# A stick-breaking and forgetting attention, pipelined head by head on one Trainium2 core

## The chip, the cores and the metric

The kernel is one program on one core of a Trainium2 chip. The metric is the device time of one execution in microseconds; less is better. All data are f32.

## The reference

Two transformer blocks run one after the other on 512 tokens of width 1024. The change lies in the attention part of the first block, which is this, cut to what matters:

```python
proj = h @ w_in                  # 8 stick-breaking and 8 forgetting heads of width 64
# stick-breaking head, query block i, keys 0..end
z = q @ k.T * HEAD_DIM ** -0.5
log_keep = where(k < q, log_sigmoid(-z), 0)
later = reverse_cumsum(log_keep) - log_keep
w = where(k < q, exp(log_sigmoid(z) + later), 0)
out = w @ v
# forgetting head: q and k are first rms-normed over the head and scaled by g_q, g_k
z = q @ k.T * HEAD_DIM ** -0.5 + log_f_cum[q] - log_f_cum[k]
out = softmax(where(k <= q, z, -inf)) @ v
x = x + (1 + ga2) * (concat(heads) @ w_o)
```

`log_f_cum` is the running sum of `log_sigmoid(h @ w_f + b_f)`, one row per head. Before this part stands a feed-forward (ffn 0), behind it another (ffn 1); the second block has linear and latent attention and a mixture of experts.

## The kernel before

The normed tokens lie feature-major in `hT` (8 chunks of 128 features x 512 tokens). Each engine has its own program, written out in order; semaphores join them, and nothing but that order and the semaphores sets when work runs. Weights come through six slots of 128x4096 (`slot0` to `slot5`), which SyncE fills in its own order as each slot is freed.

The attention goes by pairs of heads: four stick-breaking pairs, then four forgetting pairs, as two loops of three rounds and one written-out round each. A pair's q, k and v weights take one slot: slot 2 for all stick pairs, slot 3 for all forgetting pairs. Per pair TensorE makes

- q and k (`qk_projection`, L758, 8 products of 512 columns each, into banks 7 and 6 of the accumulator memory `ps`), for the next pair while the second head of a pair is worked on;
- v (L792, 32 products of 128 columns, bank 7), during the first head;

and per head

- the scores of the four query blocks against keys 0..end (L784; banks 0 to 2, 128, 256, 384 and 512 columns). In a forgetting head each of the four is followed by a second product of the same columns that adds the gate sums (L786: rows of ones and of `Fc`, in `FL` and `FR`), and by one of 128 columns that adds the causal mask (L787, the table `after` through the identity);
- ten 128x128 transposes of the weights (L804, banks 3 to 5), copied to `PT` by VectorE (L1602, L1638) and ScalarE (L1255, L1272);
- ten products with v (L820, bank 6), copied to `oT` by VectorE (L1609, L1644).

Between scores and transposes stands, in a stick head, ScalarE's abs, exp, log (L1240 to L1245), VectorE's max, scan and subtract (L1584 to L1596) and ScalarE's exp (L1249, from then on `probs_ready`); in a forgetting head, VectorE's four maxima (L1618), ScalarE's four exps (L1266) and VectorE's reciprocal and four scalings (L1621, L1626). One product of `head_ones` each for q and k (L764, L809), ScalarE's root (L1233), VectorE's reciprocal (L1569) and scaling (L1574) norm q and k of a forgetting pair; all scratch of it is in `buf1`, and q and k have one buffer each (`qT`, `kT`).

Ahead of the pairs the gate projection runs (L832), and all engines meet behind it; they meet again behind the last pair. Then come eight output chunks (L851, 8 products of 512 columns each), each added to `xT` by VectorE (L1657), with the square sums of the next norm between them (L662), and ffn 1 begins (L707).

Of the kernel before, what the change touches and what calls it, by code (L numbers as in the profile page):

```python
# [13 lines left out]
P = 128  # L14
D = 1024
KC = D // P
# [115 lines left out]
def build(nc, a, out):  # L132
    ctx = ExitStack()
    with ctx:
# [38 lines left out]
        qT = part(0, 512)  # L173
        kT = part(512, 512)
        vt = part(1024, 512).rearrange("p (t n) -> p t n", t=4)
        buf1 = part(1536, TRI)
        buf2 = part(1536 + TRI, TRI)
        PT = part(1536 + 2 * TRI, TRI).rearrange("p (b q) -> p b q", q=P)
        oT = part(5376, 4096).rearrange("p (c t) -> p c t", c=8)
        FL = big[:, 9472:9984]  # L180
        FR = big[:, 9984:10496]
        Fc = big[0:8, 10496:11008]
        fA = tmp[0:8, 0, 0:512]
        fB = tmp[0:8, 1, 0:512]
# [29 lines left out]
        s_rs = sem("rstd_ready")  # L214
# [8 lines left out]
        s_qkv = sem("qkv_done")  # L223
        s_qc = sem("q_copied")
        s_kvc = sem("kv_copied")
        s_qsq = sem("qk_squares_ready")
        s_qss = sem("qk_square_sum_done")
        s_qr = sem("qk_rstd_ready")
# [12 lines left out]
        s_fl = sem("forget_ready")  # L241
        s_fm = sem("forget_head_ready")
        s_fp = sem("forget_proj_done")
        s_f1 = sem("forget_exp_ready")
        s_wo = sem("mix_done")
# [253 lines left out]
        def _(sp):  # L499
# [54 lines left out]
            def pairs(s, at):  # L554
                k = u.take(s, 3, 4)[1]
                view = ring[s][:, 0:KC * 384].rearrange("p (k w n) -> p k w n", k=KC, w=3)
                with sp.Fori(0, 4) as i:
                    sp.wait_ge(freed[s], i + k)
                    for w in range(3):
                        sp.dma_start(view[:, :, w], w_in[:, :, bass.ds(at + w * 512 + i * P, P)]).then_inc(filled[s], 16)  # L560

            ffn(0)
            pairs(2, 0)
            pairs(3, 1536)
            for n, s in enumerate((4, 5)):
                sp.wait_ge(freed[s], u.take(s, 1)[1])
                sp.dma_start(ring[s][:, :].rearrange("p (f n) -> p f n", f=4), w_o[:, 4 * n:4 * n + 4, :])\
                    .then_inc(filled[s], 16)
            ffn(1)
# [67 lines left out]
        def _(pe):  # L637
# [111 lines left out]
            def qk_projection(s, have, i, fox, heads):  # L749

                w = ring[s][:, 0:KC * 384].rearrange("p (k w n) -> p k w n", k=KC, w=3)
                pe.wait_ge(filled[s], have + 48 + i * 48)
                for m in range(2):
                    if m == 1:

                        pe.wait_ge(s_o, heads)
                    for k in range(KC):
                        last = mm(ps[:, 7 - m, :], w[:, k, m, :], hT[:, k, META:TOK], start=(k == 0), stop=(k == KC - 1))  # L758
                    last.then_inc(s_qkv, 1)
                if fox:  # L760

                    pe.wait_ge(s_qc, i + 5)
                    pe.wait_ge(s_qsq, 2 * i + 1)
                    mm(ps[:, 7, :], const("head_ones"), buf1[:, 0:512], start=True, stop=True).then_inc(s_qss, 1)  # L764

            def pair(s, have, i, fox, after):

                w = ring[s][:, 0:KC * 384].rearrange("p (k w n) -> p k w n", k=KC, w=3)
                h0 = i * 2 + (8 if fox else 0)
                pr = i + (4 if fox else 0)  # L770
                if fox:
                    pe.wait_ge(s_qn, 2 * i + 2)
                else:
                    pe.wait_ge(s_qc, pr + 1)
                    pe.wait_ge(s_kvc, pr * 2 + 1)
                for hh in range(2):
                    h = h0 + hh
                    lo = hh * HD
                    if fox:
                        pe.wait_ge(s_fm, 2 * i + hh + 1)  # L780
                    for t in range(4):
                        n = P * (t + 1)
                        z = ps[:, [0, 0, 1, 2][t], (P if t == 1 else 0):(P if t == 1 else 0) + n]
                        last = mm(z, qT[lo:lo + HD, t * P:(t + 1) * P], kT[lo:lo + HD, 0:n], start=True, stop=not fox)  # L784
                        if fox:
                            mm(z, FL[lo:lo + HD, t * P:(t + 1) * P], FR[lo:lo + HD, 0:n], start=False, stop=True)  # L786
                            last = mm(z[:, t * P:n], ident, const("after"), start=False, stop=True, skip_group_check=True)  # L787
                    last.then_inc(s_z, 1)
                    if hh == 0:
                        for t in range(4):  # L790
                            for k in range(KC):
                                last = mm(ps[:, 7, t * P:(t + 1) * P], hT[:, k, META + t * P:META + (t + 1) * P], w[:, k, 2, :],  # L792
                                          start=(k == 0), stop=(k == KC - 1))
                        last.then_inc(s_qkv, 1)
                        pe.drain().then_inc(freed[s], 1)
                    elif after:

                        qk_projection(*after, h0 + 2)
                    pe.wait_ge(s_p, h + 1)
                    for (q, k), b in BLOCK_AT.items():  # L800
                        at = TILE_AT[q] + k * P
                        dst = ps[:, 3, b * P:(b + 1) * P] if b < 4 else \
                            ps[:, 4 + (b - 4) // 3, (b - 4) % 3 * P:(b - 4) % 3 * P + P]
                        last = nc.tensor.transpose(dst, buf2[:, at:at + P], ident)  # L804
                    last.then_inc(s_pt, 1)
                    if hh == 1 and after and after[3]:
                        pe.wait_ge(s_qsq, 2 * after[2] + 2)
                        pe.wait_ge(s_qstd, 2 * after[2] + 1)
                        mm(ps[:, 7, :], const("head_ones"), buf1[:, 512:1024], start=True, stop=True).then_inc(s_qss, 1)  # L809
                    pe.wait_ge(s_ptc, 2 * h + 2)  # L810
                    if hh == 0:

                        pe.wait_ge(s_kvc, pr * 2 + 2)
                    elif after:

                        pe.wait_ge(s_kvc, pr * 2 + 3)
                    pe.wait_ge(s_o, h + 1)
                    for q in range(4):
                        for k in range(q + 1):
                            last = mm(ps[0:HD, 6, q * P:(q + 1) * P], vt[:, k, lo:lo + HD], PT[:, BLOCK_AT[q, k], :],  # L820
                                      start=(k == 0), stop=(k == q))
                    last.then_inc(s_pv, 1)

# [4 lines left out]

            pe.wait_ge(s_late, 48)
            for k in range(KC):  # L830
                pe.wait_ge(s_hn, KC + k + 1)
                last = mm(ps[0:8, 5, :], wf[:, k, :], hT[:, k, META:TOK], start=(k == 0), stop=(k == KC - 1))  # L832
# [16 lines left out]
            for d in range(KC):  # L849
# [3 lines left out]
                if d >= 2:  # L853

                    norm_sum(2, d - 2)
# [1179 lines left out]
```

## Time and profile before

| | us |
|---|---|
| three runs: lowest, median, highest | 2963.74, 2965.77, 2982.33 |
| the profiled execution, its own time | 2963.49 |
| its span, first to last instruction | 2961.1 |
| TensorE busy | 2585.0 (87%) |
| VectorE busy | 1045.7 (35%) |
| ScalarE busy | 453.6 (15%) |
| GpSimd busy | 179.8 (6%) |
| first product behind the norm ahead of attention | at 543.06 |
| first score product | at 567.14 |
| first output product | at 958.49 |
| first product of ffn 1 | at 1026.87 |

The rows further down are of this one execution. A time of TensorE in a timeline row is the start of the first of xN products and the length to the modelled end of the last; the next row's start tells how long a group really held the engine. A product of one program line is two MATMUL records in f32. The granted clock is 1.00 where the engine ran at 2.4 GHz and 0.50 where it ran at 1.2 GHz.

### The profile page before, as it was taken

How to read it: one execution, taken by the hardware profiler on the slowest of the kernel's cores; microseconds unless marked ns; L12 is line 12 of the kernel's file. 1: busy time of each engine (PE TensorE's matmuls, PEld its weight loads, DVE VectorE, ACT ScalarE, POOL GpSimd, SP SyncE). 2: the span in 40 equal slices, each digit the busy share in tenths (PEclk: the TensorE clock that was granted, in tenths of full speed). 3: DMA queues.
4: the chain of work that ended last, by engine and by line, in shares of the span. 5: the costliest groups of instructions: out<-in, count | busy, mean ns of one | idle time of the engine just before them, and what ended most of it. 6: DMA issues, size and time to landing. Idle time of an engine off the chain costs nothing. (4 is left out here: it accounts for less than half of the span.)

```text
span 2961.1 us, 25080 instructions
## 1 busy us (share of the span) xinstructions
PE 2585.0 (87%) x9179; PEld 1222.8 (41%) x9179; DVE 1045.7 (35%) x1216; ACT 453.6 (15%) x713; POOL 179.8 (6%) x458
## 2 busy tenths in 40 slices
PE   8999999888888999999999789588888888888884
PEld 4444444455565344443444545433333333333331
DVE  3555520333333133331012662433333233233334
ACT  2000000344112100100010221011111111111111
POOL 0000000000000000000000000011111111111111
PEclk9999999998888999999999789799899999899997
DMA  7444532001013012231220100299999999999996
GB/s 260 162 135 155 172 112 61 21 25 39 22 43 113 1 57 85 63 109 39 87 101 29 33 1 22 87 416 415 416 409 411 413 402 412 407 404 415 404 409 241
DMA packets 182825, 563.10 MB, mean 190 GB/s; under 512 B 16864, under 2 KB 132848, under 8 KB 156544
## 3 DMA queue, kind: packets, MB, share of 16 engines
q1 hardware_dynamic: 172384, 554.10, 49.0%
q0 software_dynamic: 10400, 8.42, 0.9%
q8 instruction: 30, 0.49, 0.1%
q14 instruction: 11, 0.09, 0.0%
HBM read 567.19 MB, written 20.97 MB: 199 GB/s over the span
## 5 line engine op out<-in xcount | busy, mean ns | idle before, releaser
L1090 PE MATMUL ps<-slot,xT 128*64 128x512 f32 x2048 | 518.9, 665 | 160.4 <-DMA slot<-in_expert_w_up 159.4
L707 PE MATMUL ps<-hT,slot 128*128 128x512 f32 x1408 | 614.0, 597 | 13.0 <-ACT hT L1184 7.2
L707 PEld LDWEIGHTS ps<-hT,slot 128*128 128x128 f32 x1408 | 267.3, 191 | 351.1 <-issue 348.2
L1090 PEld LDWEIGHTS ps<-slot,xT 128*64 128x64 f32 x2048 | 168.6, 152 | 508.8 <-issue 459.5
L735 PE MATMUL ps<-big,slot 128*128 128x512 f32 x704 | 309.8, 600 | 12.0 <-DVE big L1499 6.2
L1918 DVE COPY hT<-ps 128x256 f32<-128x256 f32 x64 | 27.2, 424 | 630.5 <-PE ps L1098 630.5
L1109 PE MATMUL ps<-slot,hT 128*64 128x512 f32 x1024 | 233.8, 598 | 1.2 <-DVE hT L1918 1.2
L1909 DVE RECIPROCAL xT<-xT 64x512 f32<-64x512 f32 x64 | 214.1, 3345 | 2.2
L735 PEld LDWEIGHTS ps<-big,slot 128*128 128x128 f32 x704 | 135.3, 193 | 182.0 <-issue 168.9
L1495 DVE RECIPROCAL eb<-eb 128x512 f32<-128x512 f32 x44 | 147.5, 3353 | 1.5
L1493 DVE TENSOR_SCALAR eb<-eb 128x512 f32<-128x512 f32 x44 | 18.8, 427 | 331.4 <-ACT eb L1194 331.4
L1378 ACT ACTIVATE xT<-ps 64x512 f32<-64x512 f32 x64 | 37.8, 591 | 596.9 <-PE ps L1090 596.9
L1522 DVE SCALAR_TENSOR_TENSOR xT<-ps,small,xT 128x512 f32<-128x512 f32 x16 | 12.0, 750 | 296.1 <-PE ps L735 296.1
L1972 POOL MEMSET spare<- 1x4 f32 x1 | 0.1, 91 | 1915.8 <-DVEq L456 1915.8
L1109 PEld LDWEIGHTS ps<-slot,hT 128*64 128x64 f32 x1024 | 68.2, 136 | 114.9 <-issue 110.8
L758 PE MATMUL ps<-hT,slot 128*128 128x512 f32 x256 | 111.7, 594 | 0.1
L1384 ACT ACTIVATE hT<-ps 64x512 f32<-64x512 f32 x128 | 75.9, 593 | 201.5 <-PE ps L1109 200.7
L1194 ACT ACTIVATE eb<-ps 128x512 f32<-128x512 f32 x44 | 26.3, 597 | 418.6 <-PE ps L707 418.5
L1171 ACT ACTIVATE tmp<-xT 128x512 f32<-128x512 f32 (+1 forms) x32 | 20.1, 632 | 387.3 <-DVE xT L1522 327.7
L1072 PE MATMUL ps<-cst,xT 64*128 64x64 f32 x512 | 67.1, 272 | 7.5 <-DMA xT<-normed_tokens,tcol 7.5
L758 PEld LDWEIGHTS ps<-hT,slot 128*128 128x128 f32 x256 | 48.0, 190 | 61.5 <-issue 61.5
L820 PE MATMUL ps<-big 128*64 128x128 f32 x320 | 52.9, 339 | 21.5 <-DVE big L1638 8.8
(339 smaller groups left out, 2414.2 us busy)
## 6 DMA issues: line engine op xcount, KB each, us to landing
slot<-in_expert_w_gate SPq DMA_DIRECT2D x64, 2048.0 KB, 17.3
slot<-in_expert_w_up SPq DMA_DIRECT2D x64, 2048.0 KB, 22.5
slot<-in_expert_w_down SPq DMA_DIRECT2D x64, 2048.0 KB, 23.2
slot<-in_w_mod SPq DMA_DIRECT2D x18, 2048.0 KB, 8.0
slot<-in_w_gate SPq DMA_DIRECT2D x22, 1024.0 KB, 5.5
slot<-in_w_up SPq DMA_DIRECT2D x22, 1024.0 KB, 7.9
slot<-in_w_down SPq DMA_DIRECT2D x16, 1408.0 KB, 7.4
slot<-in_w_in SPq DMA_DIRECT2D x24, 512.0 KB, 5.8
```

Source lines behind the costliest of these rows:

```text
L707: last = mm(ps[:, 2 * j + g, :], w[:, g, k, j * P:(j + 1) * P], hT[:, k, META:TOK], start=(k == 0), stop=(k == KC - 1))
L735: last = mm(ps[:, down_bank(d), :], w[:, f, :], aT[:, f, :], start=(f == 0), stop=(f == FC - 1))
L758: last = mm(ps[:, 7 - m, :], w[:, k, m, :], hT[:, k, META:TOK], start=(k == 0), stop=(k == KC - 1))
L820: last = mm(ps[0:HD, 6, q * P:(q + 1) * P], vt[:, k, lo:lo + HD], PT[:, BLOCK_AT[q, k], :], start=(k == 0), stop=(k == q))
L1072: last = nc.tensor.transpose(ps[:, 4 + j, k * CAP:(k + 1) * CAP], xs[j].rearrange("p (m k) -> p k m", k=KC)[:, k, :], ident[0:CAP, 0:CAP])
L1090: last = mm(ps[g * CAP:(g + 1) * CAP, j, :], xsT[j][:, k, :], w[g][:, k, :], start=(k == 0), stop=(k == KC - 1))
L1109: last = mm(ps[g * CAP:(g + 1) * CAP, 2 + j, :], hid[j][:, c, :], w[:, c, g * 512:(g + 1) * 512], start=(c == 0), stop=(c == 3))
L1378: av(sg[j], ps[0:CAP, j, :], ACT.Exp, scale=-1.0).then_inc(s_eg, 1)
L1384: last = av(ys[j][:, g * 512:(g + 1) * 512], ps[g * CAP:(g + 1) * CAP, 2 + j, :], ACT.Copy)
L1495: v.reciprocal(eb[:, j, :], eb[:, j, :]).then_inc(s_vec, 1)
L1909: v.reciprocal(sg[j], sg[j]).then_inc(s_vec, 1)
L1918: v.tensor_copy(hid[j].rearrange("p c s -> p (c s)"), ps[:, 6 + j, 0:4 * CAP]).then_inc(s_hd, 1)
```

## The change

1. TensorE's order goes by heads: transposes of head h, scores of head h+1, products with v of head h, then half of the projections of a coming pair (`first_half` after an odd head, `second_half` after an even one). All sixteen heads are written out; there are no loops left.
2. q, k and v have two buffers each (`qb`, `kb`, `vt`, and `qF`, `kF` in slot 0). ScalarE copies them all. Pairs use slots 2, 1 and 3 in turn.
3. A forgetting head's `qF` and `kF` have 72 rows: 64 of q or k, and 8 of ones or of `Fc` times a column of the identity. The second score product is gone; the mask product stays. q and k are normed from `tmp` with scratch in `eb`, VectorE writing the two heads of a pair apart.
4. The first four of the eight products of output chunks 0 to 5 run in heads 13 and 14 and are added to `xT` there; behind head 15 come chunks 6 and 7 whole and the other four products of 0 to 5.
5. The gate projection stands behind the first scores. The meetings of all engines ahead of the pairs and behind them are gone. Maxima and exps of a forgetting head go tile by tile from the largest, each with its own signal.

The diff, cut to its core:

```diff
+        PAIR_SLOT = [2, 1, 3, 2, 1, 3, 2, 1]
+        MIX_ORDER = (6, 7, 0, 1, 2, 3, 4, 5)
...
-                        last = mm(z, qT[lo:lo + HD, t * P:(t + 1) * P], kT[lo:lo + HD, 0:n], start=True, stop=not fox)
-                        if fox:
-                            mm(z, FL[lo:lo + HD, t * P:(t + 1) * P], FR[lo:lo + HD, 0:n], start=False, stop=True)
-                            last = mm(z[:, t * P:n], ident, const("after"), start=False, stop=True, skip_group_check=True)
...
+            def scores(h):
...
+                else:
+                    pe.wait_ge(s_qn, 2 * (p - 4) + 2)
+                    pe.wait_ge(s_fm, h - 7)
+                    q, k = qF[p % 2][hh], kF[p % 2][hh]
+                for t in range(4):
+                    n = P * (t + 1)
+                    b, at = Z_AT[t]
+                    last = mm(ps[:, b, at:at + n], q[:, t * P:(t + 1) * P], k[:, 0:n], start=True, stop=True)
+                    if p >= 4:
+                        last = mm(ps[:, b, at + t * P:at + n], ident, const("after"), start=False, stop=True, skip_group_check=True)
+                last.then_inc(s_z, 1)
...
+            def first_half(n, heads):
+                pe.wait_ge(filled[PAIR_SLOT[n]], pair_have[n])
+                if n < 4:
+                    pe.wait_ge(s_qc if n == 1 else s_kc, 1 if n == 1 else n)
+                    project(n, 1, 7, 0, 4)
+                    if heads:
+                        pe.wait_ge(s_o, heads + 1)
+                    project(n, 0, 6).then_inc(s_q, 1)
+                else:
...
+                    project(n, 0, 7).then_inc(s_q, 1)
+                    pe.wait_ge(s_o, heads + 1)
+                    project(n, 1, 6).then_inc(s_k, 1)
+                    pe.wait_ge(s_qsq, 2 * (n - 4) + 1)
+                    pe.wait_ge(s_qc, n + 1)
+                    mm(ps[:, 7, :], const("head_ones"), eb[:, 0, :], start=True, stop=True).then_inc(s_qss, 1)
...
+            def second_half(n, heads):
+                if n < 4:
+                    project(n, 1, 7, 4, KC).then_inc(s_k, 1)
+                else:
+                    pe.wait_ge(s_qsq, 2 * (n - 4) + 2)
+                    pe.wait_ge(s_qstd, 2 * (n - 4) + 1)
+                    mm(ps[:, 7, :], const("head_ones"), eb[:, 1, :], start=True, stop=True).then_inc(s_qss, 1)
+                pe.wait_ge(s_o, heads + 1)
+                values(n, 6)
...
+            for h in range(N_HEAD):
+                p = h // 2
+                turn(h)
+                if h + 1 < N_HEAD:
+                    scores(h + 1)
+                else:
+                    pe.drain().then_inc(freed[0], 1)
+                head_out(h)
+                if h % 2 and p + 2 < N_PAIR:
+                    first_half(p + 2, h + 1)
+                elif not h % 2 and p + 1 < N_PAIR:
+                    second_half(p + 1, h + 1)
+                elif h < 15:
...
+                        mix(d, bank, 0, 4).then_inc(s_wo, 1)
...
+            for j, d in enumerate(MIX_ORDER):
+                mix(d, j, 0 if d >= 6 else 4, 8).then_inc(s_wo, 1)
```

VectorE's new order, by head:

```diff
+            for h in range(N_HEAD):
+                p, n = h // 2, h + 1
+                turned_out(h)
+                if n < 8:
+                    head_copy(h)
+                    log_weights(n)
+                if h % 2 == 0 and 4 <= p + 1 < N_PAIR:
+                    inverse(p + 1, 0)
+                if n >= 8:
+                    if n < N_HEAD:
+                        masked_max(n)
+                    head_copy(h)
+                    if n < N_HEAD:
+                        forget_probs(n)
...
+                if h % 2 == 0 and 4 <= p + 1 < N_PAIR:
+                    normed(p + 1, 0)
+                    inverse(p + 1, 1)
+                    normed(p + 1, 1)
```

TensorE's order in the loop over stick pairs, before. L784 are scores, L792 v, L804 transposes, L820 products with v, L758 q and k of the next pair:

```order
L792 MATMUL ps<-slot2,hT 128x128 x32
L804 MATMUL ps<-cst,big 128x128 [waits probs_ready]
L804 MATMUL ps<-cst,big 128x128 x9
...
L820 MATMUL ps<-big 64x128 [waits heads_copied,kv_copied]
L820 MATMUL ps<-big 64x128 x9
L784 MATMUL ps<-big 128x128
L784 MATMUL ps<-big 128x256
L784 MATMUL ps<-big 128x384
L784 MATMUL ps<-big 128x512
...
L758 MATMUL ps<-hT,slot2 128x512 [waits filled2]
```

And of the change, from the transposes of head 1 on (L802 transposes, L791 scores of head 2, L820 products with v of head 1, L767 half of k and all of q of pair 2):

```order
L802 MATMUL ps<-cst,big 128x128 [waits probs_ready]
L802 MATMUL ps<-cst,big 128x128 x9
L791 MATMUL ps<-slot 128x128 [waits k_copied,q_copied]
L791 MATMUL ps<-slot 128x256
L791 MATMUL ps<-slot 128x384
L791 MATMUL ps<-slot 128x512
L820 MATMUL ps<-big 64x128 [waits v_copied,probs_turned_copied]
L820 MATMUL ps<-big 64x128 x9
L767 MATMUL ps<-hT,slot 128x512 [waits k_copied,filled3]
L767 MATMUL ps<-hT,slot 128x512 x3
L767 MATMUL ps<-hT,slot 128x512 [waits heads_copied]
L767 MATMUL ps<-hT,slot 128x512 x7
```

The scores have moved from behind the products with v to ahead of them, and every head now has projections between its scores and its transposes.

VectorE's order from the work on head 7's weights to the maxima of head 8, in the change (L1611 to L1619 are `log_weights(7)`, L1649 and L1656 norm q and k of pair 4, L1638 and L1645 are copies of head 7's transposes and output, L1625 the maxima of head 8):

```order
L1611 SCALAR_TENSOR_TENSOR big<-ps,big 128x768 [waits softplus_ready]
L1614 SCALAR_TENSOR_TENSOR big<-ps,big 128x512
L1616 SCALAR_TENSOR_TENSOR big<-cst,big 128x1280 [waits vector_step]
L1617 TENSOR_TENSOR big<-ps,big 128x768 [waits vector_step]
L1619 TENSOR_TENSOR big<-ps,big 128x512
L1649 RECIPROCAL eb<-eb 128x512 [waits qk_std_ready]
L1656 SCALAR_TENSOR_TENSOR slot<-tmp,gqs,eb 64x512 [waits q_copied,vector_step]
L1656 SCALAR_TENSOR_TENSOR slot<-tmp,gqs,eb 64x512
L1649 RECIPROCAL eb<-eb 128x512 [waits qk_std_ready]
L1656 SCALAR_TENSOR_TENSOR slot<-tmp,cols,eb 64x512 [waits k_copied,vector_step]
L1656 SCALAR_TENSOR_TENSOR slot<-tmp,cols,eb 64x512
L1638 TENSOR_TENSOR big<-ps,cst 128x512 [waits probs_turned]
```

Before, the norms of this pair stood behind the copy of head 7's transposes; now they stand ahead of it, and each scaling is two instructions of 64 rows in the place of one of 128.

## Rows read from the trace of the kernel before

**Rows 1.** Busy time of each engine in four stretches, with TensorE's granted clock (PEclk).

```profile
core 0: us, PE busy (x) PEld busy (x) DVE busy (x) ACT busy (x) POOL busy (x), PEclk, DMA share, GB/s
567.10:697.80 130.70, 108.18 (x517) 75.06 (x517) 47.02 (x47) 55.28 (x53) 0.00 (x0) 0.90 0.19 48
749.10:957.50 208.40, 182.07 (x796) 120.94 (x796) 70.85 (x121) 40.31 (x93) 0.00 (x0) 0.86 0.20 63
...
749.10:771.20 22.10, 21.84 (x88) 15.69 (x88) 4.89 (x13) 2.15 (x8) 0.00 (x0) 0.62 0.00 1
775.90:797.20 21.30, 21.30 (x60) 10.17 (x60) 5.36 (x13) 3.23 (x10) 0.00 (x0) 1.00 0.12 29
```

**Rows 2.** Waits of TensorE from 552 to 1018: us in total, times, longest.

```profile
PE ps L804 <- ACT big L1249: 21.1, 4, 5.3
...
PE ps L784 <- DVE big L1574: 6.0, 3, 4.8
...
PE ps L804 <- issue: 0.8, 3, 0.3
```

**Rows 3.** Timeline of TensorE: gate projection, then the first stick pair.

```profile
543.06 9.19 PE L832 MATMUL ps<-hT,wf 128*8 128x512 f32 x16 [5.83 <-ACT hT L1184]
...
567.14 2.42 PE L784 MATMUL ps<-big 64*128 64x128 f32 x8 [0.79 <-DVE big L1560]
569.49 7.41 PE L792 MATMUL ps<-slot,hT 128*128 128x128 f32 x64
582.17 2.40 PE L804 MATMUL ps<-cst,big 128*128 128x128 f32 x10 [5.27 <-ACT big L1249]
585.65 3.71 PE L820 MATMUL ps<-big 128*64 128x128 f32 x20 [1.09 <-ACT big L1255]
589.29 2.42 PE L784 MATMUL ps<-big 64*128 64x128 f32 x8
```

**Rows 4.** Timeline of VectorE and ScalarE in head 0's chain.

```profile
574.81 0.96 DVE L1584 SCALAR_TENSOR_TENSOR big<-ps,big 128x768 f32<-128x768 f32 x1 [7.73 <-ACT big L1245]
...
580.85 1.27 ACT L1249 ACTIVATE big<-big 128x1280 f32<-128x1280 f32 x1 [4.77 <-DVE big L1596]
```

**Rows 5.** Timeline of TensorE around a forgetting head's scores.

```profile
749.13 0.79 PE L784 MATMUL ps<-big 64*128 64x128 f32 x2 [4.79 <-DVE big L1574]
...
773.62 2.37 PE L820 MATMUL ps<-big 128*64 128x128 f32 x20 [1.10 <-ACT big L1272]
775.91 0.48 PE L784 MATMUL ps<-big 64*128 64x128 f32 x2
...
782.59 13.90 PE L758 MATMUL ps<-hT,slot 128*128 128x512 f32 x32
796.32 1.02 PE L764 MATMUL ps<-big,cst 128*128 128x512 f32 x2
797.18 1.25 PE L804 MATMUL ps<-cst,big 128*128 128x128 f32 x10
```

**Rows 6.** Groups between 540 and 1045: busy us, mean ns; idle before.

```profile
L792 PEld LDWEIGHTS ps<-slot,hT 128*128 128x128 f32 x512 | 61.1, 201 | 3.0 <-issue 3.0
...
L1569 DVE RECIPROCAL big<-big 128x512 f32<-128x512 f32 x8 | 26.8, 3349 | 8.7 <-ACT big L1233 8.7
...
L1574 DVE SCALAR_TENSOR_TENSOR big<-big,gqs 128x512 f32<-128x512 f32 x4 | 3.0, 739 | 0.0
```

**Rows 7.** Timeline of VectorE: the last step of head 9's weights.

```profile
786.90 1.28 DVE L1626 TENSOR_SCALAR big<-big,fox_s 128x128 f32<-128x128 f32 x4
```

**Rows 8.** Timeline of TensorE: the outputs' start and that of ffn 1.

```profile
958.49 20.86 PE L851 MATMUL ps<-big,slot 128*128 128x512 f32 x48 [0.88 <-DVEq L456]
...
1026.87 30.32 PE L707 MATMUL ps<-hT,slot 128*128 128x512 f32 x64 [5.83 <-ACT hT L1184]
```

**Rows 9.** DMA queues of instructions, 552 to 1018, and a wait without releaser.

```profile
q8 instruction: 7, 0.11, 0.1%
q14 instruction: 3, 0.02, 0.0%
...
PEld ps L784 <- issue: 10.4, 20, 5.0
```

More of the change, by code:

```diff
@@ L568, in _ @@
                     .then_inc(filled[s], 16)
+            u.take(0, 0)
             ffn(1)
@@ new lines, in mix @@
+            def mix(d, bank, f0, f1):
+                for f in range(f0, f1):
+                    if f == 7:
+                        pe.wait_ge(s_o, N_HEAD + 1)
+                    last = mm(ps[:, bank, :], wo[f // 4][:, f % 4, d * P:(d + 1) * P], oT[:, f, :], start=(f == f0), stop=(f == f1 - 1))
+                return last
+            pe.wait_ge(filled[PAIR_SLOT[0]], pair_have[0])
+            for k in range(KC):
+                pe.wait_ge(s_hn, KC + k + 1)
+                last = mm(ps[:, 7, :], pair_w[0][:, k, 0, :], hT[:, k, META:TOK], start=(k == 0), stop=(k == KC - 1))
@@ L846, in _ @@
-            for n, s in enumerate((4, 5)):
-                pe.wait_ge(filled[s], u.take(s, 1)[0] + 16)
-            phase_left(pe, 7)
-            for d in range(KC):
-                for f in range(8):
-                    last = mm(ps[:, d, :], wo[f // 4][:, f % 4, d * P:(d + 1) * P], oT[:, f, :], start=(f == 0), stop=(f == 7))
-                last.then_inc(s_wo, 1)
-                if d >= 2:
-                    norm_sum(2, d - 2)
+            first_half(1, 0)
+            pe.wait_ge(s_f1, 1)
@@ L1284, in _ @@
+            for n in (5, 6, 7):
+                phase_left(act, n)
             norm(2)
@@ new lines, in inverse, with normed @@
+            def inverse(p, m):
+                dve.wait_ge(s_qstd, 2 * (p - 4) + m + 1)
+                link(v.reciprocal(eb[:, m, :], eb[:, m, :]))
+            def normed(p, m):
+                dve.wait_ge((s_qc, s_kc)[m], p + 1)
+                g = (gqs[:, p - 4:p - 3], col("g_k", p - 4))[m]
+                for hh in range(2):
+                    rows = slice(hh * HD, (hh + 1) * HD)
+                    last = v.scalar_tensor_tensor(out=(qF, kF)[m][p % 2][hh][0:HD, :], in0=raw[m][rows, :], scalar=g[rows, :],
+                                                  in1=eb[rows, m, :], op0=ALU.mult, op1=ALU.mult)
+                last.then_inc(s_qn, 1)
@@ new lines, in forget_rows, with mix_part @@
+            def forget_rows(p):
+                if p < 6:
+                    for hh in range(2):
+                        v.memset(qF[p % 2][hh][HD:72, :], 1.0)
+                for hh in range(2):
+                    v.tensor_scalar(kF[p % 2][hh][HD:72, :], Fc, ident[0:8, 2 * (p - 4) + hh:2 * (p - 4) + hh + 1], None, ALU.mult)\
+                        .then_inc(s_fm, 1)
+            def mix_part(d):
+                dve.wait_ge(s_wo, d + 1)
+                v.scalar_tensor_tensor(out=xT[:, d, META:TOK], in0=ps[:, 7 - (d % 3) % 2, :], scalar=gate[1][:, d:d + 1],
+                                       in1=xT[:, d, META:TOK], op0=ALU.mult, op1=ALU.add).then_inc(s_wp, 1)
@@ L1658, in _ @@
+            for n in (5, 6):
+                phase_left(dve, n)
+            dve.wait_ge(s_wp, 6)
+            for j, k in enumerate(MIX_ORDER):
+                dve.wait_ge(s_wo, 6 + j + 1)
+                v.scalar_tensor_tensor(out=xT[:, k, META:TOK], in0=ps[:, j, :], scalar=gate[1][:, k:k + 1],
                                        in1=xT[:, k, META:TOK], op0=ALU.mult, op1=ALU.add).then_inc(s_xu, 1)
```

505 lines of the change are left out of this document (227 added, 278 removed).

## The prediction

> **What bounds the kernel now.** I read the page's busy times first, then the stretches of the attention, TensorE's waits there, and its timeline. TensorE is the engine to follow: from the gate projection at 543.06 to the first product of ffn 1 at 1026.87 [rows 3, 8] lie 483.8 us, and only what shortens that stretch counts; behind it nothing is changed.
>
> Three losses stand in it. TensorE's waits add up to 62.8 us in ten groups, of which [rows 2] gives the first, one in the middle and the last. The largest is the chain of a pair's first head: scores end at 569.49, the exp that makes the weights runs at 580.85, the transposes start at 582.17; v covers 7.4 of these 12.7 us [rows 3, 4]. Second, the clock: a granted 0.90 over 130.7 us and 0.86 over 208.4 us [rows 1] are 13 and 29 us. It falls behind waits: after one of 4.79 us [rows 5] the stretch from 749.1 ran at 0.62, while 775.9 to 797.2, which had no such wait, had 1.00 [rows 1]. Third, a forgetting head's scores hold TensorE from 775.91 to 782.59, 6.7 us [rows 5], against 2.35 in a stick head [rows 3]; one of the products more per tile is the gate's, as wide as the score, so 2.35 of these are its own, 8 x 2.35 = 19 us. Together 62.8 + 42 + 19 = 124 us: what the change could win at the very most, bar what it moves under cover elsewhere.
>
> **The sum.** Pieces of TensorE's work at the full clock, start to start: transposes T 1.2 (modelled end 1.25), products with v O 773.62 to 775.91 = 2.3, q and k together 782.59 to 796.32 = 13.7, one `head_ones` product 0.9, all [rows 5]; stick scores S 2.35, v 7.4 [rows 3]; new forgetting scores F = 6.7 - 2.35 = 4.3, the mask kept. Half of k is 3.4, half of k and all of q 10.3, and three output half-chunks (12 of the 16 products in 13.7) are 10.3 too.
>
> The chain from the end of scores to transposes is 12.7 us for a stick head [rows 3]. For a forgetting head it is 5.6: scores end at 782.59, VectorE's last scaling ends at 786.90 + 1.28 [rows 5, 7]. A head now takes the larger of TensorE's work and T + scores + chain.
>
> - Lead-in. The q products are paced by ScalarE as the gate projection was, 9.3 [rows 3]; then k 6.9, v 7.4, S 2.35, gate projection 6.9, half 10.3: 43.2 us. Head 0's chain (12.7) hides behind the last two (17.2).
> - Heads 0, 2, 4: T + S + O + 3.4 + 7.4 = 16.65. Heads 1, 3: work 16.15, chain 1.2 + 2.35 + 12.7 = 16.25, so 16.25. Five of them: 82.5. ScalarE's copies of q, k and v, and VectorE's of `oT`, fall into the chain's own waits (VectorE waits 7.73 us for ScalarE, ScalarE 4.77 for VectorE [rows 4]); without that cover each 0.6 to 0.7 us copy would go straight into the 16.25.
> - Head 5: T + S + O + 13.7 + 0.9 = 20.4. Head 6: the chain, 16.25.
> - Head 7, where a stall goes in. VectorE's order puts two reciprocals (3.35 each) and four scalings (0.74 each, taken the same for 64 rows; I have no row of that shape) [rows 6] behind `log_weights(7)`: 9.7 us. It comes free for them S + 11.4 = 13.7 us after the end of head 6's transposes (11.4 from 569.49 to 580.85), and is done at 23.4, while head 7's transposes end at 16.25. The scores of head 8 wait for `qk_normed`, and behind them on TensorE stand head 7's products with v and pair 5's q and k: a stall of 7.2 us, longer than the 4.79 that it replaces. The clock falls with it. The price of that is bounded by 22.1 x (1 - 0.62) = 8.4 us [rows 1] and by 2.40 - 1.25 plus 3.71 - 2.37 = 2.5 us, from the wait of 5.27 [rows 3, 5]. I take 5: scores follow, as behind the one, but then dense q and k. So T + 7.2 + F + O + 13.7 + 0.9 + 5 = 34.6.
> - Heads 8, 10, 12: T + F + O + 0.9 + 7.4 = 16.1 each, 48.3. Heads 9, 11: T + F + O + 13.7 + 0.9 = 22.4 each, 44.8. The chain 5.6 is covered by 10.6 at least, even with a reciprocal ahead of the maxima. From the end of an even head's transposes, `qk_normed` comes at F + 5.6 + 6.4 (two scalings, reciprocal, two scalings) = 16.3 us; TensorE wants it at 14.9 + T = 16.1. That fits to 0.2 us and has no reserve.
> - Heads 13, 14: T + F + O + 10.3 = 18.1 each, 36.2. VectorE's six added sums there cost nothing; they stand behind the weights of the next head, with 10.3 us of products as cover.
> - Head 15: T, 1.1 for the copies of the transposes [rows 5], O: 4.6.
> - The rest. Before, 1026.87 - 958.49 = 68.4 [rows 8]. Six half-chunks are gone from it, 24 products = 20.6: 47.8. The norm behind them is as before.
>
> Sum: 43.2 + 82.5 + 20.4 + 16.25 + 34.6 + 48.3 + 44.8 + 36.2 + 4.6 + 47.8 = 378.7 us, 105 less than 483.8. The seams between groups cost more than these rows hold in some places; I allow 0.25 us in each head, 4 us, bounded by 0 and by the 0.79 that TensorE waited for a copy just made [rows 3], 13 us. That leaves 101. From above it agrees: 124 less the new stall and its clock (12) is 112.
>
> Moved without a price: weights of a pair land some microseconds behind their issue and are asked for two pairs ahead, and slots 0 and 1 come free for ffn 1 at heads 15 and 12, with 47.8 us or more before it begins. If a fill were late there, ffn 1 would wait once, by a few us.
>
> The profiled execution took 2963.5, so 2862.5; the median of three is 2.3 above it: **2865**.
>
> **A rule weighed.** The gate rows make the score products 72 rows high. Of TensorE's weight loads [rows 6] has 201 ns each for v's products, yet 64 products took 7.41 us [rows 3], less than their loads laid end to end (12.9), though all use all 128 rows: loads overlap products there. The Trainium skill, "TensorE: Matmul & The Clock Gate", section "The mechanism", says that a load overlaps matmuls in flight only when its row group differs. By that rule v could not run as it does; the trace disagrees, and I take F as it stands.
>
> **Rivals.**
>
> 1. VectorE becomes the bound in the forgetting pairs (0.2). For it: the 0.2 us above, and in-order copies that hang behind the norms. Against it: tile by tile maxima and exps shorten the 5.6. It decides from a wait of about 3 us: then the clock falls too. Three such heads (10, 12, 14) at 3 + 5 each are 24 us: 77 saved, 2889.
> 2. The 72-row scores lose the overlap of their loads (0.05). Eight loads per head x 8 heads x 201 ns [rows 6] = 13 us: 2878. This is the rule above, as it would act here.
> 3. The pipeline does not do what it says in the stick heads (0.07): ScalarE, in order, takes a copy or a root late, and the chain grows by 4 us, in eight heads, with TensorE idle for it but little clock lost: 32 us, 69 saved, 2897.
> 4. Code loading makes it slower (0.03). The loops are gone; four written bodies become eight, and the ten fetches of instructions in the stretch [rows 9] at most twenty. If each stopped TensorE by 5.0, the longest of its waits there without releaser [rows 9], and cost 2.5 of clock, 20 x 7.5 = 150 us are lost, 49 more than won: 3014. It decides from 5.05 us per fetch. Against it: ten fetches passed with 0.3 us as the longest such wait of a product [rows 2].
> 5. The stall of head 7 costs less than I think and every seam is free (0.1): 4 + 5 and some of the 7.2: 114 saved, 2852.
>
> **How the numbers follow.** The forecast, 2855 to 2876, has 0.5; the remaining 0.05 is for mishaps unnamed, on either side. With 2 in 10 left out, the range reaches over rivals 5, 2 and 1 and most of 3: 2848 to 2898. Its ends are also the bounds: 105 + 9 saved below, and above 13 of seams, 8.4 of clock and 24 for rival 1. A run of this kernel differs from the next by up to 1% or so; 1% is 30 us, and only rival 4 and a mishap stand above 2936. Faster by over 1% 0.95, within 1% 0.02, slower by over 1% 0.03.
>
> **What would show it.** Right: TensorE's waits in the attention fall from 62.8 to some 15 us, one of them of about 7 before head 8's scores, released by VectorE's scaling of k; granted clock near 0.97 outside of it; stick heads 16 to 17 us apart; forgetting pairs 38 to 39 apart; ffn 1 starts near 926. Wrong: waits of over 2 us at every second forgetting head's scores (rival 1), at every stick head's transposes (rival 3), gaps without releaser (rival 4), or F well over 4.3 at a full clock (rival 2).

## The result and the profile after

The changed kernel takes 2857.1 us (median of four runs, 2856.7 to 2857.5) where the kernel before took 2967.3 (four runs, 2963.7 to 2982.3): a ratio of 0.9631, 95% interval 0.9616 to 0.9646. That is 110 us saved; the forecast was 2865, 101 less than the 2965.8 that was known then. The profiled execution took 2857.5, its span is 2855.6.

First the page after, its section on busy times.

```profile
PE 2528.6 (89%) x9115; PEld 1178.5 (41%) x9115; DVE 1040.7 (36%) x1204; ACT 466.1 (16%) x732; POOL 179.7 (6%) x458
```

TensorE is busy 56 us less, and 49 us of its idle time are gone. Two stretches of the attention, stick heads and forgetting heads, in the columns of [rows 1]:

```profile
586.00:700.00 114.00, 113.68 (x584) 75.67 (x583) 49.16 (x51) 66.12 (x70) 0.00 (x0) 1.00 0.16 42
740.00:840.00 100.00, 98.24 (x552) 70.21 (x551) 56.27 (x86) 44.16 (x85) 0.00 (x0) 1.00 0.00 1
```

TensorE is now busy for all but 0.3 us of 114, and the granted clock is 1.00 in both, where [rows 1] had 0.90 and 0.86. TensorE's waits from 543 to 920, as [rows 2] had them (L791 scores, L802 transposes, L773 v, L820 products with v, L860 output; left out are the 5.8 of the first q product and of ffn 1 and 0.2 just ahead of ffn 1, which were there before as well):

```profile
PE ps L791 <- DVE slot L1656: 6.4, 1, 6.4
...
PE ps L802 <- ACT big L1312: 3.4, 1, 3.4
PE ps L773 <- DVE big L1645: 1.4, 3, 0.5
PE ps L820 <- ACT big L1333: 0.9, 1, 0.9
PE ps L860 <- issue: 0.3, 1, 0.3
PE ps L791 <- issue: 0.3, 1, 0.3
```

They add up to 12.7 us, against 62.8. TensorE's timeline shows the attention's start, a stick pair, the one stall left (heads 6 to 8), a forgetting head's scores and the end, beside [rows 3, 5, 8] (the number behind a time is the group's length; L767 is q and k, L842 and L850 `head_ones`, L793 the mask):

```profile
544.85 9.33 PE L866 MATMUL ps<-hT,slot 128*128 128x512 f32 x16 [5.83 <-ACT hT L1240]
...
588.14 1.25 PE L802 MATMUL ps<-cst,big 128*128 128x128 f32 x10
589.33 2.42 PE L791 MATMUL ps<-slot 64*128 64x128 f32 x8
591.68 2.40 PE L820 MATMUL ps<-big 128*64 128x128 f32 x20
...
604.96 1.31 PE L802 MATMUL ps<-cst,big 128*128 128x128 f32 x10
...
709.37 2.06 PE L802 MATMUL ps<-cst,big 128*128 128x128 f32 x10 [3.37 <-ACT big L1312]
717.79 0.80 PE L791 MATMUL ps<-slot 72*128 72x128 f32 x2 [6.36 <-DVE slot L1656]
...
724.07 3.73 PE L820 MATMUL ps<-big 128*64 128x128 f32 x20
...
743.51 0.39 PE L791 MATMUL ps<-slot 72*128 72x128 f32 x2
743.73 0.39 PE L793 MATMUL ps<-cst 128*128 128x128 f32 x2
...
746.66 2.40 PE L820 MATMUL ps<-big 128*64 128x128 f32 x20
748.99 1.12 PE L850 MATMUL ps<-eb,cst 128*128 128x512 f32 x2
750.59 7.41 PE L773 MATMUL ps<-slot,hT 128*128 128x128 f32 x64 [0.48 <-DVE big L1645]
...
871.03 17.43 PE L860 MATMUL ps<-big,slot 128*128 128x512 f32 x40 [0.33 <-issue]
...
918.81 30.68 PE L715 MATMUL ps<-hT,slot 128*128 128x512 f32 x64 [5.83 <-ACT hT L1240]
```

From 544.85 to 918.81 lie 374.0 us; before they were 483.8 [rows 3, 8]. That difference, 109.8, is more than the whole difference of the two profiled executions (106.0): this one of the change took 1.8 us longer ahead of the stretch and 2.6 longer behind it. "Stretch" below is always this one, from the first q product (before: gate projection) to ffn 1. What lies outside of it varies by some us from one execution to the next, so stretches of profiles tell small differences better than medians, which are given too. A stretch is of one execution each.

### The profile page after: what moved, and what is told of

The parts are those of the page before. It is cut to its first block and busy times, and to the rows that moved or that the text cites. A ratio compares the mean times of both kernels' runs of the same rounds, so it can differ in the third digit from the quotient of the medians.

```text
span 2855.6 us, 24702 instructions
## 1 busy us (share of the span) xinstructions
PE 2528.6 (89%) x9115; PEld 1178.5 (41%) x9115; DVE 1040.7 (36%) x1204; ACT 466.1 (16%) x732; POOL 179.7 (6%) x458
## 5 line engine op out<-in xcount | busy, mean ns | idle before, releaser
L1145 PEld LDWEIGHTS ps<-slot,xT 128*64 128x64 f32 x2048 | 156.2, 152 | 521.7 <-issue 306.7
L767 PE MATMUL ps<-hT,slot 128*128 128x512 f32 x240 | 105.8, 596 | 0.0
L767 PEld LDWEIGHTS ps<-hT,slot 128*128 128x128 f32 x240 | 44.8, 190 | 55.0 <-issue 55.0
L2024 POOL DMA_INDIRECT xT<-normed_tokens,tcol x66 | 64.4, 975 | 34.0 <-issue 34.0
## 6 DMA issues: line engine op xcount, KB each, us to landing
slot<-in_w_mod SPq DMA_DIRECT2D x18, 2048.0 KB, 16.9
```

The lines of the kernel that those rows point to most:

```text
L767: last = mm(ps[:, bank, :], pair_w[p][:, k, m, :], hT[:, k, META:TOK], start=(k == 0), stop=(k == KC - 1))
L1145: last = mm(ps[g * CAP:(g + 1) * CAP, j, :], xsT[j][:, k, :], w[g][:, k, :], start=(k == 0), stop=(k == KC - 1))
L2024: pool.indirect_dma_start(xs[j], None, u_dram, bass.IndirectOffsetOnAxis(tcol[j][:, :], 0), bounds_check=SEQ - 1, oob_is_err=False).then_i ...
```

## The experiments

Each is the changed kernel (2857.1, stretch 374.0) with one edit.

**The gate as a product of its own, of 8 rows.**

```diff
-  last = mm(ps[:, b, at:at + n], q[:, t * P:(t + 1) * P], k[:, 0:n], start=True, stop=True)
...
+  mm(ps[:, b, at:at + n], q[0:HD, t * P:(t + 1) * P], k[0:HD, 0:n], start=True, stop=False)
+  mm(ps[:, b, at:at + n], q[HD:72, t * P:(t + 1) * P], k[HD:72, 0:n], start=False, stop=True)
```

> The gate rows stay in qF and kF, but go through a product of their own (8 rows) behind the 64-row score product, as before the change. The changed kernel holds TensorE for 3.15 us with a forgetting head's scores, where I had predicted 4.3 by taking only the gate product's 2.35 off the old 6.7. Theory A (the second product brought more than its columns; mixing products of different row counts costs TensorE at each switch): scores go back to 6 to 6.7 us, 8 x 3.2 = 23 to 28 us in all, so about 2883 us. Rival B (a product costs its columns, whatever stands beside it): 8 x 2.15 = 17 us, about 2874 us, scores at 5.3 us.

2926.2 us (2923.5 to 2929.9), ratio to before 0.9863 (0.9847 to 0.988), stretch 443.8: 70 more than the change, and far above both theories (2883 and 2874). Head 9's scores in its timeline (L794 64 rows, L795 8 rows, L796 mask):

```profile
751.51 0.48 PE L794 MATMUL ps<-slot 64*128 64x128 f32 x2
751.92 0.48 PE L795 MATMUL ps<-slot 8*128 8x128 f32 x2
752.34 0.49 PE L796 MATMUL ps<-cst 128*128 128x128 f32 x2
752.75 0.70 PE L794 MATMUL ps<-slot 64*128 64x256 f32 x2
...
756.52 2.03 PE L794 MATMUL ps<-slot 64*128 64x512 f32 x2
```

Start to start, a product of 128 columns takes 0.41, 0.42 and 0.41 us here; in the change 0.22 each. And at 756.52 the products run at half clock with no wait ahead of them. The window of this kernel:

```profile
740.00:840.00 100.00, 99.78 (x385) 59.92 (x383) 34.12 (x48) 28.00 (x50) 0.00 (x0) 0.82 0.00 1
```

TensorE is busy 99.8% of the time and has 0.82. So the edit measures two things, product time and clock; the next three runs go after them one by one.

**Gate products of 64 rows, as before the change.** Its `FL` and `FR` are of 64 rows again, in buffers of their own:

```diff
+  mm(ps[:, b, at:at + n], q[0:HD, t * P:(t + 1) * P], k[0:HD, 0:n], start=True, stop=False)
+  mm(ps[:, b, at:at + n], FL[hh], FR[p % 2][:, 0:n], start=False, stop=True)
...
```

> The gate's own product again, now as before the change: 64 rows (8 of them not zero) in separate buffers, behind the 64-row product of q and k; the order by heads stays. Theory A (a narrow product of few used rows also counts less for the clock): scores 6.7 us at the full clock as before the change, eight heads 28 us, and a further 10 to 40 us for stretches at half the clock: 2895 to 2925 us. Rival B (only the 8-row form costs clock): 2885 us. Rival C (my prediction's price, the gate product's columns alone, 19 us): 2876 us.

2889.8 (2887.2 to 2891.6), 0.9745 (0.9729 to 0.9761), stretch 404.6: 30.6 more than the change, with the clock at 1.00 from 740 to 840:

```profile
749.26 0.48 PE L796 MATMUL ps<-slot 64*128 64x128 f32 x2
749.58 0.38 PE L797 MATMUL ps<-big 64*128 64x128 f32 x2
749.90 0.49 PE L798 MATMUL ps<-cst 128*128 128x128 f32 x2
...
756.02 2.40 PE L825 MATMUL ps<-big 128*64 128x128 f32 x20
```

A head's scores take 749.26 to 756.02 = 6.76 us, which is the 6.7 of [rows 5]. This is what the gate rows are worth in this kernel: 31 to 33 us. The clock that the run before lost goes with its 8-row products and not with a product of the gate's own. Two things differ between the two: the height, and the rows where the product lies (64 to 71 there, 0 to 63 here). No run parts them.

**Scores of 64 rows, the gate sums left out.**

```diff
-  q, k = qF[p % 2][hh], kF[p % 2][hh]
+  q, k = qF[p % 2][hh][0:HD, :], kF[p % 2][hh][0:HD, :]
```

> Forgetting heads' scores use rows 0 to 63 of qF and kF alone, so the gate sums are left out of the scores; mask product and everything else as in the change. Fewer rows are multiplied. The run with a product of 8 rows between products of 64 and 128 rows took 0.41 us for each 128-column product where the change takes 0.22, and lost half its clock without any wait. Theory A (each switch between a 64-row and a 128-row product costs about 0.2 us of TensorE, while 72 and 128 rows count as the same): scores take 3.15 + 8 x 0.2 = 4.75 us instead of 3.15, eight heads 13 us, so 2870 us although less is computed. Rival B (only products of very few rows cost that): no difference, 2857 us.

2865.0 (2864.5 to 2865.4), 0.9662 (0.9646 to 0.9679), stretch 385.6, 11.7 more, clock 1.00. The same products and columns as in the change, eight rows fewer, and dearer (in the medians by 7.9 us; theory A had 13):

```profile
746.46 0.48 PE L791 MATMUL ps<-slot 64*128 64x128 f32 x2
746.87 0.49 PE L793 MATMUL ps<-cst 128*128 128x128 f32 x2
...
751.06 2.40 PE L820 MATMUL ps<-big 128*64 128x128 f32 x20
```

0.41 and 0.42 in the place of 0.22 and 0.23; a head's scores take 4.60 against 3.15. Eight changes between 64 and 128 rows lie in them, 0.18 us for each.

**The 72-row product made twice, the scores thus doubled.**

```diff
-  last = mm(ps[:, b, at:at + n], q[:, t * P:(t + 1) * P], k[:, 0:n], start=True, stop=True)
+  last = mm(ps[:, b, at:at + n], q[:, t * P:(t + 1) * P], k[:, 0:n], start=True, stop=p < 4)
...
+  mm(ps[:, b, at:at + n], q[:, t * P:(t + 1) * P], k[:, 0:n], start=False, stop=True)
```

> Each forgetting score product of 72 rows runs twice (the scores are doubled), mask as before: the same number and width of products as with the gate's own product, but all of 72 or 128 rows. Theory A (the 69 us that the separate 8-row gate product cost are mostly its row count, by switches and by the clock): scores take 3.15 + 2.15 = 5.3 us, eight heads 17 us, granted clock as in the change: 2874 to 2876 us. Rival B (any third product per tile brings the half clock, whatever its rows): 2900 us or more.

2876.0 (2873.9 to 2881.0), 0.9705 (0.9689 to 0.9721), stretch 390.8, 16.9 more, clock 1.00.

```profile
746.22 0.39 PE L791 MATMUL ps<-slot 72*128 72x128 f32 x2
...
751.53 2.40 PE L821 MATMUL ps<-big 128*64 128x128 f32 x20
```

A head's scores take 5.31 us. The columns of a second product cost 5.31 - 3.15 = 2.16 per head, and at the same columns the form with 64 rows costs 6.76 - 5.31 = 1.45 more, again eight changes of 0.18. So of the gate rows' worth 17 us are columns, and most of the rest, 8 x 1.45 = 12, goes with the changing between 64 and 128 rows, which the change removed as well: products of 72 rows beside those of 128 take 0.22 us for 128 columns each, with nothing on top.

It is the turn-taking and not the 64 rows as such: a stick head's four score products, 64 rows and no mask between them, take 2.35 us [rows 3], and the same columns with 72 rows and no mask take 2.25 (the run without the mask, below). With the mask between them the two forms are 1.45 us apart.

The Trainium skill, "TensorEngine Tiling (Array Packing)", section "Key Properties", says that changing the tiling mode, not just the tile, drains the engine; the page lists 64 rows as one mode and the full 128 as another. The runs fit that rule, at 0.18 us for each change, if 72 rows count as the full height. That TensorE drains there they don't show.

**Scores behind the products with v.**

```diff
   turn(h)
-  if h + 1 < N_HEAD:
-      scores(h + 1)
...
   head_out(h)
+  if h + 1 < N_HEAD:
+      scores(h + 1)
```

> TensorE's order is put back to products with v of head h, then scores of head h+1; projections stay halved and every head has its half. Theory A (the chain of 12.7 us per stick head must find 12.7 us of work between scores and transposes): cover falls from 12.9 to 10.5 us, and products with v now wait 1.1 us for the copies of the transposes: a stick head takes 1.2 + 1.1 + 2.3 + 2.35 + 12.7 = 19.7 instead of 16.6, eight heads 24 us, forgetting heads 1.1 us each for the copies, 9 us; the waits of 2.2 us leave the clock up: 2885 to 2892 us. Rival B (what counts is only that each head has a projection beside it): under 10 us slower, 2867 us at most.

2895.0 (2890.7 to 2899.5), 0.9761 (0.9743 to 0.9778), stretch 416.3, 42.3 more. Its waits, and a stick head:

```profile
PE ps L820 <- issue: 24.2, 15, 6.8
PE ps L802 <- ACT big L1312: 13.6, 5, 5.7
```

```profile
624.95 1.97 PE L802 MATMUL ps<-cst,big 128*128 128x128 f32 x10 [2.12 <-ACT big L1312]
627.87 4.50 PE L820 MATMUL ps<-big 128*64 128x128 f32 x20 [0.95 <-issue]
```

The products with v stand right behind the transposes and wait there in each head: 0.95 us in eleven heads, 1.97 in four, and 6.80 in head 7, where VectorE's norms stand ahead of its copy. The profile names no releaser but in the last; by the program's order they wait for the copies of the transposes. The scores, and so the weights of the next head, are then late (2.12 at the next transposes). Behind the two waits the products with v run at half clock, 4.50 against 2.40. The waits are 44.0 us in all, 31 more than in the change; clock (0.90 from 586 to 700) is most of the rest. Up to head 6's transposes, so in the stick heads, 24.5 of the 42.3 us are lost. The first two stick heads take 19.5 and 19.6 us, where the theory of an exposed chain had 19.7; that the clock would fall with waits this short it didn't expect, and 2895 lies above its 2885 to 2892.

**k whole, not in halves.**

```diff
-  project(n, 1, 7, 0, 4)
+  project(n, 1, 7).then_inc(s_k, 1)
...
-  if n < 4:
-      project(n, 1, 7, 4, KC).then_inc(s_k, 1)
-  else:
+  if n >= 4:
```

> For stick pairs 2 and 3 (and pair 1 in the lead-in) the k products stand whole at the odd head, none at the even one, so odd heads have 13.7 us of projections and even ones 7.4 instead of 10.3 and 10.8. Theory A (the chain of 12.7 us needs its cover in each head, not on average): even heads go from 16.8 to 16.3 us with TensorE idle for 3 us, odd ones from 16.3 to 19.6; three pairs, about 3 x 2.9 = 9 us, and 2 to 3 us of clock behind each of three waits: 2866 to 2874 us. Rival B (three waits of 3 us leave the clock up): 2864 us. Rival C (the spread of the projections does not matter, their sum does): 2857 us.

2872.2 (2864.1 to 2875.4), 0.9673 (0.9657 to 0.9688), stretch 390.7, 16.7 more, as its theory A had it (2866 to 2874). An even stick head has 7.4 us of projections for cover now instead of 10.9, and waits:

```profile
641.67 1.43 PE L802 MATMUL ps<-cst,big 128*128 128x128 f32 x10 [2.09 <-ACT big L1310]
643.04 4.63 PE L791 MATMUL ps<-slot 64*128 64x128 f32 x8
647.60 4.53 PE L820 MATMUL ps<-big 128*64 128x128 f32 x20
```

From the end of the scores to these transposes lie 12.7 us in the first such head, the chain that the prediction took from [rows 3]. There are three waits of 2.09 or 2.10; behind the first the clock stayed up, behind the other two scores and products with v took 9.0 and 7.9 us in the place of 4.7. The price of waits of this length is paid now and then, which may be why this kernel's runs lie 11 us apart.

**Outputs whole, behind head 15.**

```diff
-  for d in range(3 * (h - 13), 3 * (h - 13) + 3):
...
-      mix(d, bank, 0, 4).then_inc(s_wo, 1)
...
-  mix(d, j, 0 if d >= 6 else 4, 8).then_inc(s_wo, 1)
+  mix(d, j, 0, 8).then_inc(s_wo, 1)
```

> All eight output chunks run whole behind the last head, none in heads 13 and 14. 20.6 us of products move to the end. Theory A (the halves are worth what they cover): heads 13 and 14 become bound by the chain, T + F + 5.3 = 9.7 us each instead of 17.0, so 14.6 us come back, with two waits of some 3 us and their clock (2 to 5 us) lost: 8 to 11 us slower, 2865 to 2868 us. Rival B (the chain of the last heads is short enough to be free, or the waits leave the clock alone): 6 us slower or less, 2863 us. Rival C (the extra sums on VectorE cost as much as is won): no difference, 2857 us.

2859.3 (2858.1 to 2861.0), 0.9638 (0.9622 to 0.9654), stretch 379.0, 5.0 more: two waits for the weights of heads 14 and 15, and a clock that stays up behind both. That is rival B (6 us or less).

```profile
842.51 1.28 PE L802 MATMUL ps<-cst,big 128*128 128x128 f32 x10 [2.39 <-DVE big L1626]
...
851.35 1.31 PE L802 MATMUL ps<-cst,big 128*128 128x128 f32 x10 [2.17 <-DVE big L1626]
```

The output halves in the last heads are thus worth about 5 us by the stretch and 2.2 by the medians, the least of the parts.

**The mask product left out.**

```diff
-  if p >= 4:
-      last = mm(ps[:, b, at + t * P:at + n], ident, const("after"), start=False, stop=True, skip_group_check=True)
```

> The causal mask of the forgetting heads is left out (four products of 128 columns per head are gone, and heads see later keys). Theory A (TensorE bounds every forgetting head, and a mask product between 72-row products costs its 0.22 us and nothing else): scores 3.15 - 4 x 0.22 = 2.25 us, eight heads 7 us, 0.9 of it at half the clock in head 8: 2849 to 2850 us. Rival B (the chains or VectorE's norms take over, since TensorE comes to the next scores 0.9 us sooner than qk_normed): under 4 us, 2853 us or more.

2855.3 (2854.3 to 2857.2), 0.9627 (0.9612 to 0.9641), stretch 369.4, 4.5 less. Each head's scores are 0.9 us shorter (2.25 against 3.15), 7.2 in all, but part of it turns into a wait:

```profile
742.52 2.32 PE L791 MATMUL ps<-slot 72*128 72x128 f32 x8
```

```profile
PE ps L773 <- DVE big L1643: 4.1, 3, 1.4
```

This wait was 1.4 in all with the mask: 2.7 us come back. VectorE's copy of the head's output stands behind a reciprocal of 3.35 us and the maxima, and v waits for it. So VectorE is close behind TensorE in the forgetting pairs. The median shows only 1.8 of the 4.5, which this measurement can hardly tell from nothing.

**q of pair 5 ahead of head 8's scores**, where the stall is.

```diff
-  project(n, 0, 7).then_inc(s_q, 1)
+  if n != 5:
+      project(n, 0, 7).then_inc(s_q, 1)
...
   turn(h)
+  if h == 7:
+      pe.wait_ge(filled[PAIR_SLOT[5]], pair_have[5])
+      pe.wait_ge(s_qstd, 2)
+      project(5, 0, 7).then_inc(s_q, 1)
   if h + 1 < N_HEAD:
```

> The q products of pair 5 (6.9 us) are moved from behind head 7's products with v to ahead of head 8's scores, where TensorE waits 6.36 us for the norms of pair 4. Theory A (that wait and the half clock behind it, 3.1 us in the scores and 1.3 in the products with v, are on the path): the wait goes and the clock stays up, 6.4 + 4.4 = 10.8 us faster, 2846 to 2848 us. Rival B (something else then holds head 8, such as ScalarE's or VectorE's chain behind scores that start no earlier): under 4 us, 2853 us or more. Rival C (the low clock comes from the 3.37 us wait ahead of head 7's transposes, not from this one): the wait goes but scores stay at half the clock, 6 to 7 us, 2850 us.

2842.7 (2842.5 to 2848.3), 0.9588 (0.9572 to 0.9604), stretch 364.7, 9.2 less (theory A: 10.8 less, 2846 to 2848; the medians are 14.4 apart).

```profile
708.27 2.14 PE L802 MATMUL ps<-cst,big 128*128 128x128 f32 x10 [3.37 <-ACT big L1317]
710.21 7.92 PE L767 MATMUL ps<-hT,slot 128*128 128x512 f32 x16
717.97 0.39 PE L791 MATMUL ps<-slot 72*128 72x128 f32 x2
```

```profile
715.14 1.51 DVE L1661 SCALAR_TENSOR_TENSOR slot<-tmp,cols,eb 64x512 f32<-64x512 f32 x2
```

From the start of head 7's transposes to the scores are 9.7 us, where the change had 8.4: VectorE's scaling of k ends at 716.65, and the scores now follow the q products, which are in part at half clock (7.76 us from start to start, where 6.9 are due). But the wait of 6.36 us is gone, 6.9 us of products are done in its place, and scores (3.15 us) and products with v run at full clock; behind them stands a new wait of 0.87 for VectorE's copy of the head.

**The stall filled whole**: half of that q ahead of head 7's transposes, where the 3.37 was, half behind them, and VectorE's first reciprocal for pair 4 ahead of `log_weights(7)`.

```diff
+  if h == 7:
...
+      project(5, 0, 7, 0, 4)
   turn(h)
+  if h == 7:
+      project(5, 0, 7, 4, KC).then_inc(s_q, 1)
...
+  if h == 6:
+      inverse(4, 0)
   log_weights(n)
```

> Pair 5's q products are split, four ahead of head 7's transposes and four ahead of head 8's scores, and VectorE makes the first reciprocal of pair 4 ahead of head 7's weights, where it waits 3.5 us for ScalarE. Theory A (both waits around heads 7 and 8, 3.37 and 6.36 us, and the half clock behind each are on the path): against the run with the q products moved whole (2842.7) the 3.37 and 0.87 us waits go, and the transposes and q products at half the clock (0.9 and 1 us) with them: 5 to 6 us, 2837 us. Rival B (the reciprocal delays head 7's chain by as much as it gains): 2840 us or more.

2842.9 (2839.7 to 2845.4), 0.9591 (0.9575 to 0.9607), stretch 360.3, 13.7 less than the change.

```profile
705.31 3.67 PE L767 MATMUL ps<-hT,slot 128*128 128x512 f32 x8 [0.26 <-issue]
708.82 1.26 PE L802 MATMUL ps<-cst,big 128*128 128x128 f32 x10
...
713.53 0.49 PE L791 MATMUL ps<-slot 72*128 72x128 f32 x2
```

Both stalls are gone; a wait of 0.87 for the copy of the head stays. Theory A had the split 5 to 6 us ahead of q moved whole, at 2837 us; the stretch is 4.4 shorter, the medians are alike. To tell the two versions apart each was run again, five times.

> The kernel with pair 5's q products moved whole ahead of head 8's scores, again, with more rounds, beside the next one on the same chip. Theory A: 2842 to 2844 us as before.

> The kernel with the q products split and the early reciprocal, again. In its profile the attention was 4.5 us shorter than that of the kernel with the q products moved whole (360.3 against 364.8 us), but the medians of four runs were alike (2842.9 and 2842.7). Theory A (the 4.5 us are real and the medians differ by what lies outside the attention from run to run): 3 to 5 us less than the other, 2838 to 2840 us. Rival B (they are given back somewhere): no difference.

2844.3 (2841.8 to 2849.0), 0.9591 (0.9578 to 0.9604), and 2843.3 (2838.7 to 2847.4), 0.9581 (0.9567 to 0.9594). The stretches were 364.7 and 360.3 again, 4.4 apart as at first; behind them lay 1932.7 and 1937.4 in the profiled executions. So theory A of the last run (2838 to 2840) came true in the stretch and not in the median. Which of the two is faster as a whole the runs don't settle. Both beat the changed kernel, by 13 to 14 us in the medians; of that 9.2 and 13.7 are in the stretches of the profiles.

## Why the prediction was right

It was, by its own steps, within 8 us; the size of the gain came out of the sum, 382.7 with the allowance against 374.0 measured.

- **Where the time goes.** The three losses were the right ones: waits went from 62.8 to 12.7, the clock to 1.00 in both stretches outside of head 7, and one product of two per tile is gone. The third was priced too low (below), so 124 us was not the bound it was called; with 31 for the gate it is 136.
- **Lead-in, stick heads.** 43.3 us (43.2 forecast). Heads 0 to 4: 16.8, 16.3, 16.8, 16.3, 16.8, in sum 83.1 (82.5). The order by heads with k in halves is what does it: with scores behind the products with v this part loses 24.5 us, with k whole 17. In head 2 the exp that makes the weights ends at 621.18 and the transposes start at 621.28: the odd stick heads have 0.1 us to spare. Head 5 was 20.6 (20.4).
- **Head 6.** 17.5 (16.25). Head 7's chain took 13.97 us, from 695.40 to 709.37, and not 12.7: behind the root of pair 4's norm ScalarE loads a table once more ahead of its exp. The same exp of heads 1 to 6 has no such load.

```profile
696.82 1.28 ACT L1307 ACT_TABLE_LOAD   x1
```

- **Head 7.** 33.1 (34.6). The named wait came: 6.36 us for VectorE's scaling of k. I had 7.2, and 5 for the clock. Measured from the rows, transposes took 0.8 more than 1.25, scores 6.28 in the place of 3.15 and products with v 1.3 more: 5.3. Of these only 4.5 stand behind the wait that I had priced, the 0.8 behind the 3.37 ahead of head 7's transposes; that 5 came out so near is luck in part, taken as it was between bounds of 2.5 and 8.4. The 64-row scalings took 1.51 for two, as taken. Removing the wait alone gave 9.2 us, and with the ScalarE wait of 3.37 as well 13.7.
- **The mis-sized term: F.** I forecast 4.3 us, and it is 746.66 - 743.51 = 3.15. In the step "2.35 of these are its own, 8 x 2.35 = 19 us" I took a stick head's 2.35 for the gate product, where all products are of 64 rows. The products in [rows 5] alternated between 64 and 128 rows as well, at 0.18 for each change by the runs above; the gate rows took this away too. The gate's worth was 31 us, not 19. In the five heads 8 to 12 that is 5.8 us; 2.1 of it went back, since an even head's `head_ones` product and the wait behind it (748.99 to 750.59) take 1.6 where I had 0.9. The 0.48 of it that waits for `oT`'s copy behind the reciprocal I hadn't named. The forgetting pairs were thus 37.0 us apart and not 38 to 39, and ffn 1 started at 918.8 and not near 926.
- **Seams.** I allowed 4 us; the seams cost 0.1 to 0.2 us a head in the stick heads and nothing that shows behind them, so it was hardly needed. This is rival 5's half that came. Without the allowance the sum was 378.7, 4.7 too long. F alone made it 9 too long in eight heads; about half of that was given back by the terms priced too low, the `head_ones` products, head 6's chain and the stick heads. That the total came so near is in part such offsetting.
- **Heads 13 and 14, head 15, the rest.** 17.0 each (18.1; F again), 4.9 (4.6) and 47.8 (47.8). The output halves are worth 5 us.
- **Rival 1, VectorE as the bound**, did not come, by a hair: the scaling of k ends at 758.99, and scores start at 759.25.

```profile
754.11 3.35 DVE L1649 RECIPROCAL eb<-eb 128x512 f32<-128x512 f32 x1
757.49 1.50 DVE L1656 SCALAR_TENSOR_TENSOR slot<-tmp,cols,eb 64x512 f32<-64x512 f32 x2
```

I had it 0.2 us too late. The longer F has no part in that, for it stands on both sides; what made room is TensorE itself, which came 0.7 us later than I had it, by the `head_ones` product and the wait above. Without the mask, so with 0.9 us less of products, VectorE's copy takes part of the gain. It is the next bound.
- **Rival 2, the loads**, fell: 72 and 128 rows side by side take 0.22 us for 128 columns, less than before. The price lay in the heights that the kernel had, not in the one that it got.
- **Rival 3** stayed away in the change (16.8 at most in heads 0 to 4), but for head 7's chain, where a root in ScalarE's order did cost 1.3 us. Scores behind the products with v, and k whole, are what it looks like. **Rival 4** stayed away: 17 fetches of instructions in the stretch where [rows 9] had 10, and 0.3 us as the longest wait of a product without releaser, as in [rows 2].

The 110 us cannot be split into a sum. Taken away one at a time, gate rows are worth 31, scores ahead of the products with v 42, k in halves 17, output halves 5. That is 95, each taken from a kernel that has the others. What the meetings of the engines, the second buffers and the maxima tile by tile gave was not tried alone.

## What to carry to other kernels

Where one engine is to be kept full, put between a result and its use the work of another head, and count for each chain what is behind it; then look for the one place where the pattern changes (here head 7, the first norm), which was worth 13 to 14 us more. Count a matmul not by its columns alone: here f32 products of 64 and of 128 rows in turn cost 0.18 us at each change, and eight rows added to the 64 took that cost away and brought none. If a forecast subtracts one group from another, both must have the same neighbours.

## What the runs showed that I had not expected

- The clock fell with no wait at all: 0.82 over 100 us at 99.8% busy with 8-row products (in rows 64 to 71) in the stream, 1.00 with 64-row products (in rows 0 to 63) in their place. Which of the two does it stays open. Over the stretch that was 70 - 31 = 39 us between the two runs, some 6 of them for four more changes of height in each of eight heads.
- Waits near 2.1 us cost the clock in some places and not in others: of the three of k whole, two; of the two in the outputs' run (2.39 and 2.17), none.
